# Weight slabs split in halves, four buffers deep, in a single-core transformer trunk

## The reference

```python
def conv_ffn(h, w_up, conv_w, w_down):
    up = causal_depthwise_conv(h @ w_up, conv_w)   # width 3
    gate, val = jnp.split(up, 2, axis=-1)
    return (jax.nn.silu(gate) * val) @ w_down

h = h + val_glu * sigmoid(gate_glu)        # (s5 output @ w_glu), 1024 -> 2048
h = h + conv_ffn(rms_norm(h), ...)         # 1024 -> 5632, 2816 -> 1024
k, v = rms_norm(h) @ w_kv                  # 1024 -> 512, once
h = h + attention(rms_norm(h) @ w_q, k, v) @ w_o
h = h + conv_ffn(rms_norm(h), ...)
```

## Time and profile before

| | us |
|---|---|
| Median of 3 runs | 1340.31 (1339.22 to 1340.93) |
| Span of the profiled execution, first to last instruction | 1338.1 |
| PE busy | 1159.8 (87%) |
| DVE, ACT, POOL busy | 752.3, 447.8, 622.9 |

### The profile page before, as it was taken

How to read it: one execution, slowest core, us unless ns; L and a number is a source line. 1 busy time by engine, 2 the same in 40 slices (tenths; PEclk the granted TensorE clock), 3 DMA queues, 4 the chain that set the end, 5 groups by cost and what they waited for, 6 DMA issues and landing times.

```text
span 1338.1 us, 25655 instructions
## 1 busy us (share of the span) xinstructions
PE 1159.8 (87%) x9938; PEld 1134.2 (85%) x9938; DVE 752.3 (56%) x1134; ACT 447.8 (33%) x763; POOL 622.9 (47%) x374
## 2 busy tenths in 40 slices
PE   1502779998999999999999989989999999999996
PEld 1402768998999999999999988889999999999996
DVE  6999986123666666664111577734666666661001
ACT  5600124224333333332222345434333333332222
POOL 1854041454454454456455434366444444455452
PEclk9656889999999999999999999999999999999998
DMA  8011004332222322323322333323223223233331
GB/s 121 1 18 18 6 14 130 85 89 78 80 79 78 94 78 78 93 85 106 91 86 75 97 82 89 73 64 90 84 79 86 87 78 88 85 96 99 97 86 63
DMA packets 217613, 103.86 MB, mean 78 GB/s; under 512 B 42245, under 2 KB 216197, under 8 KB 217493
## 3 DMA queue, kind: packets, MB, share of 16 engines
q1 hardware_dynamic: 217559, 103.12, 28.4%
HBM read 97.57 MB, written 3.18 MB: 75 GB/s over the span
## 4 chain that ended last, share of the span: by engine, by line
DVE 39%; PE 35%; issue 11%; ACT 10%; POOL 1%; DVEq 1%; DMA 1%; ACTq 1%; SPq 0%; POOLq 0%
PE slot L995 31%; DVE cbuf L1539 16%; DVE cbuf L1541 5%; ACT cbuf L708 5%; DVE ubuf L1536 2%; ACT w_hi L536 2%; PE slot L933 1%; ACT prob L795 1%; DMA xc<-in_x 1%; POOL w_lo L1758 1%; DVE pt L1629 1%; PE slot L931 1%; DVE phase L1257 1%; DVE qt L1592 1%; DVE phase L1262 1%
## 5 line engine op out<-in xcount | busy, mean ns | idle before, releaser
L1758 POOL TENSOR_TENSOR w_lo<-raw,w_hi 128x1024 fp32r<-128x1024 f32 (+1 forms) x156 | 400.3, 2566 | 348.4 <-ACT w_hi L536 317.1
L995 PE MATMUL slot<-xa_hi,w_hi 128*128 128x264 f32 (+1 forms) x1728 | 354.9, 287 | 31.2 <-POOL w_lo L1758 25.7
L995 PE MATMUL slot<-xa_hi,w_lo 128*128 128x264 f32 (+1 forms) x1728 | 351.1, 285 | 0.0
L995 PE MATMUL slot<-xa_lo,w_hi 128*128 128x264 f32 (+1 forms) x1728 | 350.8, 284 | 0.0
L1539 DVE SCALAR_TENSOR_TENSOR cbuf<-ubuf,conv_w,cbuf 128x528 f32<-128x528 f32 (+1 forms) x88 | 217.4, 2470 | 157.8 <-ACT cbuf L708 157.8
L995 PEld LDWEIGHTS slot<-xa_hi,w_hi 128*128 128x128 f32 x1728 | 268.6, 189 | 39.6 <-issue 39.2
L995 PEld LDWEIGHTS slot<-xa_lo,w_hi 128*128 128x128 f32 x1728 | 268.3, 189 | 0.0
L995 PEld LDWEIGHTS slot<-xa_hi,w_lo 128*128 128x128 f32 x1728 | 267.8, 189 | 0.0
L536 ACT ACTIVATE w_hi<-raw 128x1024 fp32r<-128x1024 f32 (+1 forms) x154 | 171.9, 1116 | 198.7 <-PE slot L995 195.4
L995 PE MATMUL slot<-act_hi,w_hi 128*128 128x264 f32 (+1 forms) x704 | 142.1, 283 | 2.8 <-POOL w_lo L1758 2.8
L995 PE MATMUL slot<-act_lo,w_hi 128*128 128x264 f32 (+1 forms) x704 | 141.6, 282 | 0.0
(11 more groups left out here) (296 smaller groups left out, 1478.4 us busy)
## 6 DMA issues: line engine op xcount, KB each, us to landing
raw<-in_ffn_w_up SPq DMA_DIRECT2D x88, 512.0 KB, 3.8
raw<-in_ffn_w_down SPq DMA_DIRECT2D x32, 704.0 KB, 4.8
raw<-in_s_w_glu SPq DMA_DIRECT2D x16, 512.0 KB, 4.0
raw<-in_w_q SPq DMA_DIRECT2D x8, 512.0 KB, 4.6
raw<-in_w_o SPq DMA_DIRECT2D x8, 512.0 KB, 4.3
xc<-in_x SPq DMA_DIRECT2D x1, 2048.0 KB
xt<-in_x SPq DMA_DIRECT2D x1, 2048.0 KB, 9.8
raw<-in_w_kv SPq DMA_DIRECT2D x4, 512.0 KB, 4.1
```

The lines of the kernel that those rows point to most:

```text
L995: ins = mm(slot[dst][:, half, 0:b - a], w[:, buf, k * P:(k + 1) * P], xx[:, k0 + k, a:b], start=opens and k == 0 and n == 0, stop=closes a ...
L1758: tt(w_lo[:, buf, 0:nk * P], raw[:, buf, 0:nk * P], f32(w_hi[:, buf, 0:nk * P]), ALU.subtract).then_inc(lo_done, 1)
```

## The change

All dense weights go in halves of a slab (*chunks*) through four buffers: 4 + 4 input tiles for a slab of 8, and 6, 6, 5, 5 for a down tile of 22. The total room of `raw`, w_hi and w_lo stays the same. `slab_used`, `hi_done` and `lo_done` now count chunks; a chunk may be split when the chunk four before it has been used. TensorE waits for a chunk when it comes to it, and marks it used at its last matmul. The places of the splits on ACT and of `low` on POOL are changed as well: before the stream copies four chunks are split; in the glu loop the gate comes ahead of the splits except on the last tile, where three or four chunks of the next stage stand before it; in the attention heads two chunks are always split, so that the w_o slabs are prepared inside the last head. Core of the diff:

```diff
+NB = 4
+KC = KD // 2
+DN = (6, 6, 5, 5)
+W_AT = (0, 6, 12, 17)
-                split_at(base, m, 2, 1, KD)
...
+                def tile(m, nxt):
                     if isinstance(m, int) and m == 0:
                         rms(before)
                     else:
-                        val_tile(m - 1 if isinstance(m, int) else act.snap(m - 1))
-                    split_at(base, m, 2, 2, n2)
+                        less = m - 1 if isinstance(m, int) else act.snap(m - 1)
+                        tap(1, less)
+                    split_at(base, m, 4, nxt[0])
+                    if not (isinstance(m, int) and m == 0):
+                        act_copy(less)
+                    split_at(base, m, 5, nxt[1])
                     gate_tile(m)
+                    split_at(base, m, 6, nxt[2])
+                    split_at(base, m, 7, nxt[3])
...
-                act.wait_ge(slab_used, s - 1)
-                run(w_hi[:, buf, 0:nk * P], raw[:, buf, 0:nk * P], ACT.Copy).then_inc(hi_done, 1)
+                act.wait_ge(slab_used, s - (NB - 1))
+                run(buffer_of(w_hi_all, buf, nk), buffer_of(raw_all, buf, nk), ACT.Copy).then_inc(hi_done, 1)
...
-                if start == 0:
-                    pe.wait_ge(hi_done, s + 1)
-                    pe.wait_ge(lo_done, s + 1)
...
+                for c, tiles_in_c in enumerate(chunks):
+                    for kc in range(tiles_in_c):
+                        if start <= k < stop:
+                            if kc == 0:
+                                pe.wait_ge(hi_done, s + (c + 1))
+                                pe.wait_ge(lo_done, s + (c + 1))
...
-                    low(m * 2 + (base + 1), 1, KD)
+                    low(m * 4 + (base + 4), 0, DN[0] if last else KC)
                     if not is0(m):
                         act_low(less(m))
-                    low(m * 2 + (base + 2), 0, KS if last else KD)
+                    for n in range(1, 4):
+                        low(m * 4 + (base + 4 + n), n, DN[n] if last else KC)
...
+            for b in range(NB):
+                act.wait_ge(raw_landed[b], 16)
+                run(buffer_of(w_hi_all, b, KC), buffer_of(raw_all, b, KC), ACT.Copy).then_inc(hi_done, 1)
...
-                    if ahead:
-                        split_at(S_Q, j, 2, 2 + par, KD)
+                    for n in range(2):
+                        split_at(S_Q, j, 4 + 2 * par + n, KC)
```

More of the change, by code:

```diff
@@ L431, in load, with half @@
                     sp.wait_ge(lo_done, split)
-                dma(raw[:, buf, 0:nk * P].rearrange("p (k c) -> p k c", k=nk), src).then_inc(raw_landed[buf], 16)
+                dma(buffer_of(raw_all, buf, nk).rearrange("p (k c) -> p k c", k=nk), src).then_inc(raw_landed[buf], 16)
+            def half(w, n, col):
+                return w[:, n * KC:(n + 1) * KC, bass.ds(col, P)]
             sp.wait_ge(win_t_ready, 8)
-            load(0, glu_v[:, :, 0:P], KD, None)
-            load(1, glu_v[:, :, D:D + P], KD, None)
+            for n in range(4):
+                load(n, half(glu_v, n % 2, n // 2 * D), KC, None)
             full_wait(sp, "y3")
@@ L454, in down @@
                     col = sp.snap(i * P)
[L455 to L457 removed]
+                    for n in range(4):
+                        split = sp.snap(i * 4 + (base + n - 3))
+                        load(n, w[:, W_AT[n]:W_AT[n] + DN[n], bass.ds(col, P)], DN[n], split)
             def one_stream(w, tiles, base):
@@ L461, in one_stream @@
                     cols = [sp.snap(i * (2 * P) + n * P) for n in range(2)]
[L462 to L467, removed]
+                    for n in range(4):
+                        split = sp.snap(i * 4 + (base + n - 3))
+                        load(n, half(w, n % 2, cols[n // 2]), KC, split)
+            two_streams(glu_v, 1, KD, D, S_GLU)
+            two_streams(up_v[0], 0, KF, FFN, S_UP0)
             down(dn_v[0], S_DN0)
             one_stream(kv_v, 4, S_KV)
-            for n in range(2):
-                load(n, q_v[:, :, n * P:(n + 1) * P], KD, S_Q + n - 1)
+            for n in range(4):
+                load(n, half(q_v, n % 2, n // 2 * P), KC, S_Q + n - 3)
             for a in range(2):
@@ L512, in _ @@
                 cols = [sp.snap(j * (2 * P) + n * P) for n in range(2)]
-                split = [sp.snap(j * 2 + (S_Q + n - 1)) for n in range(2)]
-                for n in range(2):
-                    load(n, q_v[:, :, bass.ds(cols[n], P)], KD, split[n])
+                for n in range(4):
+                    split = sp.snap(j * 4 + (S_Q + n - 3))
+                    load(n, half(q_v, n % 2, cols[n // 2]), KC, split)
                 k_load(jr, scored)
@@ L1095, in q_slab @@
                         pe.wait_ge(q_evicted, hp)
-                    slab(hp + S_Q, e, 0, xq_hi, xq_lo, ready=ready if first else None, part=part,
+                    slab(hp * 2 + S_Q, (KC, KC), 2 * e, 0, xq_hi, xq_lo, ready=ready if first else None, part=part,
                          tokens=Q_TOKENS)
@@ L1843, in tile @@
                     if not last or nxt:
-                        low(m * 2 + (base + 2), 0, nxt if last else KS)
+                        for n in range(4):
+                            low(m * 4 + (base + 4 + n), n, nxt if last else DN[n])
                 loop_2(KD, tile)
```

258 lines of the change are left out of this document (127 added, 131 removed).

## The result

| | before | after |
|---|---|---|
| median of the runs, us | 1340.62 (1339.22 to 1341.57) | 1297.58 (1296.20 to 1298.03) |
| profiled execution: time, span, us | 1340.3, 1338.1 | 1296.2, 1294.4 |
| tile of the first / second up stage, us | 12.63 / 12.51 | 11.72 / 11.48 |

The ratio is 0.9676 (0.9663 to 0.9689). The forecast was 1304, with 1296 to 1325 as its range. The span is 43.7 us shorter where the sum said 36.5. A tile is here the mean distance between the Silu of one tile and that of the next, over 14 distances from the sixth of a stage on. TensorE's own tiles after, the same 19 x 96 matmuls of each stage, are 223.19 and 219.13 us in all, 11.75 and 11.53 each. The Silus come closer at first, 11.6 us apart up to the eighth distance of the first stage and 11.75 from the ninth on: the other engines start behind TensorE and catch up.

The account below looks back on a forecast made before the run. The up loop of ACT, DVE and POOL was taken to bound the kernel, TensorE's w_lo wait its echo. Gains 31.1 + 2.6 + 2.1 + 1.3 - 0.6 = 36.5 gave span 1301.6 and time 1304 us, range 1296 to 1325.

Parts of the forecast that it names:

- (e): Up stages: TensorE sets the pace at 11.82 and 11.62 us a tile, above the 11.4 loop; 1304 us, chance 0.62.
- up term: Up stages: 19 x 0.78 + 19 x 0.86 = 31.1 us gained as TensorE's idle time per tile goes.
- Rival (a): Up stages' first tiles, 4 x 0.8 us, and more of the xa_lo waits also gain; about 1298, chance 0.10.
- hand-made loop: Up tile's ACT, DVE and POOL loop redone from Silu: 11.4 us where it was 12.6, collisions summing to 2.6.
- rival (b): Up loop: POOL's queued halves go back to back ahead of the waiting DVE operation; about 1322, chance 0.14.
- Attention and w_o: w_o halves split inside the last head remove 1.6 us of wait plus 0.5 of another 1.0: 2.1 (0 to 2.6).
- Glu to up: Handover: Sigmoid 0.54 us later, but xa_lo waits lose 1.8; net gain 1.3 us (-0.5 to 1.6).
- Start: Four splits instead of one stand before the stream copies: 0 to 1.2 us late, 0.6 taken.
- Loads at no cost: Half-slab loads of 256 KB land in about 2.5 us, before they are wanted: cost 0 (bound 5 us).
- (d): Up loop: collisions multiply, slower from 3.72 us a tile; 1363 us, chance 0.09.
- (c): No change, 1340: up-loop collisions shift but sum to 3.7 us, edges gain and lose alike; chance 0.05.

Follow-up runs that it names:

- lighter TensorE: Up stages leave out a third of their matmuls (w_hi x_lo), one execution each: kernel after 1287.26 us, kernel before 1340.68, place alone 1318.19.
- place alone: Kernel before, whole slabs, with a tile's second up split moved ahead of act_hi and its w_lo ahead of act_lo: 1304.96 us, ratio 0.9736.
- halves, old place: Kernel after, with the up loop's moved split put back behind act_hi and its w_lo behind act_lo: 1308.46 us, ratio 0.9772.
- late split: Kernel after, with the second w_o slab's halves split after the last head, as before the change: 1301.83 us, ratio 0.9697.
- mended edges: Kernel after, with one split instead of four ahead of the first stream copies and the last pre-up split behind the last Sigmoid: 1296.53 us.
- old lead: Kernel after, with ACT's split and TensorE's wait held to the times two whole slabs gave: 1303.12 us, ratio 0.9728.
- no port reads: Kernel before, with POOL's w_lo in the up stages a subtraction of 8 columns and a memset of the rest: 1299.7 us, ratio 0.9698.

## Why the prediction was right, point by point

- **TensorE sets the pace of the up stages, the forecast (e).** Right: no w_lo wait is left, TensorE is busy throughout, and the loop under it is 11.55 us where 11.4 was worked out. The kernels with a lighter TensorE show that the loop was the limit before and no longer is.
- **The size of the up term.** Too small: the two up stretches, with the starts of down in them, give 39.6 (19.3 + 20.4, rounded) where 31.1 + 2.6 were reckoned. Both traces have the same 2068 matmuls in each stretch, so the 5.9 can be placed:

| part of both stretches, us | forecast | measured |
|---|---|---|
| the 19 tiles of each | 31.1 | 34.1 (239.36 to 223.19, 237.09 to 219.13) |
| from there to the first matmul of down | 2.6 | 3.1 |
| statistics and first tiles | 0 | 2.4 |

  The step that was off most is the pace. I took it from the first matmul after a wait to the last pair, 11.82 and 11.62 a tile; TensorE's tiles are 11.75 and 11.53. The first pair after a wait takes 0.31 us to the next one where a pair takes 0.24, and that 0.07 goes with the wait:

```profile
457.75 0.41 PE L995 MATMUL slot<-xa_lo,w_hi 128*128 128x264 f32 x2
457.99 0.40 PE L995 MATMUL slot<-xa_hi,w_lo 128*128 128x264 f32 x2
459.07 0.48 PE L995 MATMUL slot<-xa_hi,w_hi 128*128 128x264 f32 x2 [0.67 <-POOL w_lo L1758]
459.38 0.28 PE L995 MATMUL slot<-xa_lo,w_hi 128*128 128x264 f32 x1
```

  Rival (a) had named the first tiles, at 3.2 us (it wrote twenty tiles counted where it was nineteen). They gave 1.0. The other 1.4 of the 2.4 are the clock: before, the granted clock is 0.50 from 338 to 341 us, behind the waits on xa_lo, and the first 24 matmuls of the statistics and after take 4.77 us instead of 3.34. The kernel after has the same fall, from 331 to 334 us, but there it lies in the glu row. That the time landed by rival (a)'s 1298 is luck, and it lies only 1.6 us inside the range.
- **The hand-made loop.** Its length was near, its order wrong in one place. It had the first multiply-add slip in between the first two halves at no loss, and then 0.9, 0.8, 0.1 and 0.8 lost. In the trace the first starts 0.07 us before the half ends, is passed over and loses 1.1; the others lose 0.9, nothing (abuf), nothing and 0.8. The sum of 2.6 was 2.87. Without TensorE's pace the loop fell from 12.55 to 11.55, by 1.00 where 1.2 was reckoned; 0.66 of it is the port's (3.37 to 2.71 us lost a tile), where 0.84 was reckoned. So the port's order is neither the forecast's "DVE always in between" nor rival (b)'s "POOL first": in this kernel each comes once a tile.
- **Halves were not needed for it.** The prediction gave the gain to both the place and the smaller collisions, and my first expectation gave place alone nothing. Place alone gives 37.8 of the 44.3 us after the first glu matmul. It does so by ACT's part of the loop, and halves by the port; the us a tile (first stage) and what the four multiply-adds lose of it:

| | before | place alone | halves, old place | after |
|---|---|---|---|---|
| tile; lost at the port | 12.63; 3.44 | 11.75; 3.31 | 12.06; 2.70 | 11.72; 2.87 |
| with a lighter TensorE | 12.55; 3.37 | 12.12; 3.80 | not run | 11.55; 2.71 |

  The terms add up: 12.63 less 0.95 and 0.13 would be 11.55 for place alone, under TensorE's 11.75, and 12.63 less 0.74, with 0.13 more for ACT's second half, is 12.02 for the halves, where 12.06 was measured. With all its matmuls TensorE hides the difference between place alone and both; with fewer it shows, 12.12 against 11.55. What the halves and their lead add to place is 6.6: 3.4 at w_o, 1.3 at K/V and the heads, 1.0 at glu, 2.2 at the up stages and the first down (1.4 of it the clock behind the statistics, which place alone has as before), less 1.3 at the end.
- **Attention and w_o.** 2.1 forecast, 4.4 measured (1.2 + 3.2). The wait of 1.6 was right; missing was the granted clock that fell behind the two waits. The shares come from the run with the late split.
- **Glu to up.** 1.3 forecast net; the waits on xa_lo lost the 1.8 foreseen. The glu row shows 1.0, but only since the stretch at granted clock 0.50, which both kernels have, moved into it from the next row: with that row's 1.4 it is 2.4. **Start.** +0.6 as forecast, but executions scatter there by more, so that agreement is worth nothing.
- **Loads at no cost.** Right: 176 loads of 256 KB land in 3.0 us (median; 2.5 was the estimate). TensorE waits for no load, and ACT for none of an up or down slab; its waits for q and w_o loads are 3.2 us in all where they were 3.4.

```profile
raw<-in_ffn_w_up SPq DMA_DIRECT2D x176, 256.0 KB, 3.0
raw<-in_ffn_w_down SPq DMA_DIRECT2D x32, 384.0 KB, 3.5
```

  By the Trainium skill, DMA: Bandwidth & Descriptors, section Anatomy of one DMA, about 2 us of a DMA are a fixed cost; the section describes DMAs that GpSimd issues, and SP issues these. The lines from 256 KB through 384 and, of the kernel before, through 512 KB leave 2.0 and 2.2 us at zero bytes, so these traces are nearer to the page's figure than to the 1.1 that I had drawn from 512 and 704 KB. It is hidden all the same.
- **Slower, (d), and no change, (c).** The collisions did spread to L1554, but summed to 2.87, well under the 3.72 from which (d) decides.

Open: the 0.5 us at the first down; whether the 1.2 us at the end belong to the change. At the end the eight matmuls of the last statistics take 1.86 us where they took 1.05, the halved pace of the lower clock, behind the same wait:

```profile
1283.35 1.86 PE L1237 MATMUL slot<-ones,acc 128*128 128x1 f32 x8 [0.81 <-POOL acc L1780]
```

The kernel with mended edges lost only 0.4 there, the one with the late w_o split 1.2, the one with the old lead nothing. That suggests chance, and no run settles it.

## What to carry to other kernels

When a wait of TensorE names a producer, follow that producer's engine round one turn: here the wait was the echo of a loop that closed without TensorE, and removing a third of TensorE's work showed it in one run. Before an operation is moved, two prices are asked: what it frees in its own engine's turn, here 0.95 us a tile, and what its successor on another engine falls on. With whole slabs the second price depended on TensorE (3.31 us a tile with all its matmuls, 3.80 with two thirds); halving the operation made it smaller in both cases. And a second wait of TensorE close behind another can cost its own length again through the clock behind it (1.6 us of wait, some 1.5 of clock), so such waits are worth more than their entry in the list.

## What was not expected of the hardware

- Less work for TensorE made a kernel slower: "place alone" has tiles of 11.75 us with all matmuls and 12.12 with two thirds of them, since buffers come free earlier and POOL's operations then fall on more of DVE's (3.80 us lost a tile instead of 3.31).
- The order at the shared port: a DVE operation that starts 0.25 us before POOL's ends goes next (0.80 us, and the POOL operation queued behind takes 1.76 for 1.29); one that starts 0.07 us before it is passed over (1.89). Over the 89 such meetings of the trace the order turns at about 0.1 us. The Trainium skill, SBUF — State Buffer, section Who interferes with whom, has issue order decide; the trace agrees if a DVE operation's claim counts from about 0.1 us after its start.
- Around w_o the granted clock fell to 0.50 for some 3.4 us where TensorE waited 1.7 us, ran nine matmuls and waited 1.6 us (the kernel before, place alone, no port reads). It stayed at 1.00 behind the 1.7 alone (the kernel after, halves in the old place) and behind 1.7 and 0.4 (late split).
- Around the waits on xa_lo it fell to 0.50 in every kernel with all matmuls, and not for the same time: 3.4 us in the kernel after and 6.8 in the one with the late w_o split, whose wait is the same 3.6 us.
